# The final norm's two sums of squares: per-block matmuls with two columns instead of running sums on VectorE

## The chip, the cores and the metric

One core of a Trainium2 chip (trn2) runs the whole kernel. The metric is the device time of that core in microseconds (us). TensorE has two clock levels, 1.2 and 2.4 GHz; the profile shows as "granted clock" which share of full speed the chip allowed.

## The reference, cut to what matters

Two networks run one after the other on 1024 tokens of width 1024, all in fp32. The first has two attention layers and ends in a norm, with the gain `final_norm_gain`. The second starts with a norm of its own (`norm_mix_g_2`) ahead of a pooling mixer and a feed-forward part (FFN).

```python
def rmsnorm(x, g):
    y = xf * lax.rsqrt(jnp.mean(xf * xf, axis=-1, keepdims=True) + EPS)
    return (y * g).astype(x.dtype)
# first_block:  x = x + y @ w_out_odd[o];   return rmsnorm(x, final_norm_gain)
# second_block: h = rms_norm(x, norm_mix_g[0]);  x = x + pool_mixer(h, ...)
#               x = x + conv_ffn(rms_norm(x, norm_ffn_g[0]), ...)
```

Two norms follow directly on each other there. With r = 1/sqrt(mean(x^2) + eps), the second norm needs mean((x r g)^2) = r^2 mean((x g)^2). So the kernel takes two sums over the features of the same x: of x^2, and of (x g)^2, with g the final gain. "The final norm" below means this pair.

## The kernel before, in words

x lies transposed in SBUF: eight blocks `X[:, c, :]` of 128 features (partitions) by 1024 tokens. Most work is done in two halves of 512 tokens, n = 0 and n = 1. The weights come by DMA (queue SP) into a raw ring `WR`; ScalarE (ACT) rounds them to a high part and GpSimd (POOL) or VectorE (DVE) takes the low part (`split`, L2357), into a ring of six slots in `WS` and, late in the kernel, four more in `PT`. Each product takes three matmuls (high x high, high x low, low x high: L1534 to L1536).

A planner in Python writes one list, `steps`; each engine's program goes through this list in its order and issues its part of each step. So an instruction on an engine is always behind the engine's parts of all earlier steps. Side work is written as generators that are advanced by one `yield` for each piece of a matmul task ("pump"); a piece is mostly 6 matmuls.

The stretch around the change is `odd_tail`:

- Eight tasks `p1{oc}0` finish the output projection for n = 0 (12 matmuls each), then eight tasks `o1{oc}1` do it for n = 1 (36 matmuls each). After each, VectorE adds the product to X (L2036). They use PSUM banks 0 and 1 in turn, so the second next task waits for that addition.
- `rows_out` calls `square(fin[n], oc, ...)` one piece after task oc. For the final norm `fin[n]` that is two ScalarE squares of a 128x512 block: plain (`PY<-X`), and with the gain as scale (`PY<-X,COL`). Block 0 goes straight to two accumulators in `PY`; for blocks 1 to 7 each square goes to one of three slots `YS` and VectorE adds it to its accumulator (step `acc`, L2173). An `acc` is held back until the next call of `square` or the end. A slot of `YS` is free again once its `acc` is done.
- `close(fin[n])`: TensorE sums each accumulator over the partitions with a column of ones (step `sums`, L1707: 16 matmuls with the 128x128 piece of squares as weights and one column moving). VectorE and GpSimd work out both roots (L2180, L2346, L2186 to L2196), TensorE spreads them (`bcast`, L1721) into banks B_S+n and B_S+n+2 (B_S = 2).
- `mixed(n)` then runs the pooling mixer's blocks 0 to 7: `block sum` (L2246, L2253 or the scan L2255), `block diff` (L2269, L2271, L2273) on VectorE, `block split` on ScalarE, `block lo` (L2416) on GpSimd. `block sum` of block c waits for `block lo` of block c-2. `mixed(0)` goes beside the tasks `o1{oc}1`, `mixed(1)` beside the first FFN tasks. The pool products (`pool mm`) are tasks of 2 pieces between them; each of the eight blocks of a half gets one more ScalarE square and an `acc` for the FFN norm `ffn[n]`.
- The FFN begins with `half_task`s (24 matmuls). Each ends in `half leave`, in which ScalarE copies two columns to `TAIL` and scales the bank to a buffer `HBUF`; buffer 0 is PY[:, 1024:1536], which is also the second accumulator of half 0. Ahead of it ScalarE waits for `p.after`, a list that has the `sums` of `fin[1]` as the planner knows it when the step is written. Next come two VectorE instructions of `half conv` (L2282, L2288). For the first `half_task`, the planner has not yet closed `fin[1]`, so the value waited for there is 0. `close(fin[1])` follows one piece later.

Other norms (`x_norm`, `l1`, `ffn`, `mem_norm`) use the same functions with one sum each (`second` is None).

Of the kernel before, what the change touches and what calls it, by code (L numbers as in the profile page):

```python
# [9 lines left out]
ALU = mybir.AluOpType  # L10
# [55 lines left out]
class Norm:  # L66


    def __init__(self, src, n, stat, base, bank, second=None):
        self.src, self.n, self.stat, self.base, self.bank, self.second = src, n, stat, base, bank, second  # L70
        self.acc = [0, 0]
        self.var2 = self.var3 = self.rstd2 = 0
        self.sums = self.var = self.rstd = self.bcast = 0
        self.nd, self.nh, self.lo = [0] * 8, [0] * 8, [0] * 8
        self.col = self.ring = self.dst = None
        self.before = []
# [86 lines left out]
def build(nc, d):  # L163
    ctx = ExitStack()
    with ctx:
        def sb(name, shape, dt=F):
            return ctx.enter_context(nc.sbuf_tensor(name, shape, dt))
# [21 lines left out]
        ST = sb("ST", [128, 8, 4])  # L189
        RD = sb("RD", [128, 2, 2, 2])  # L190
        SK = sb("SK", [128, 8])
        PCT = sb("PCT", [128, 4, 16])
        SS = sb("SS", [128, 16])
        SM = sb("SM", [128, 16])
# [87 lines left out]
        s_score, s_mx, s_exp, s_sink, s_rec = (signal(n) for n in ("s_score", "s_mx", "s_exp", "s_sink", "s_rec"))  # L282
        s_turn, s_pth, s_ptl, s_pv = (signal(n) for n in ("s_turn", "s_pth", "s_ptl", "s_pv"))
        s_spread, s_yc, s_fin = (signal(n) for n in ("s_spread", "s_yc", "s_fin"))
        s_sq, s_acc, s_sums, s_var, s_pow, s_bcast = (signal(n) for n in ("s_sq", "s_acc", "s_sums", "s_var", "s_pow", "s_bcast"))
        s_nd, s_nh, s_nlp, s_nlv = (signal(n) for n in ("s_nd", "s_nh", "s_nlp", "s_nlv"))
        s_yh, s_ylp, s_ylv = signal("s_yh"), signal("s_ylp"), signal("s_ylv")
# [310 lines left out]
        def flush_acc():  # L598
            while held:
                put("acc", *held.pop(0))  # L600

        def square(nm, c, need):
            flush_acc()
            for j in range(1 if nm.second is None else 2):
                if c == 0:
                    put("square", nm, c, j, need, None, (s_turn, s_turn.n), (s_sums, s_sums.n))
                    nm.acc[j] = (s_sq, s_sq.add())
                    continue
                i = at["ys"] % 3
                at["ys"] += 1  # L610
                put("square", nm, c, j, need, i, ys_after[i], nm.acc[j])
                held.append((nm, j, i, s_sq.add(), nm.acc[j]))
                nm.acc[j] = ys_after[i] = (s_acc, s_acc.add())

        def close(nm):
            flush_acc()
            both = nm.second is not None
            nm.sums, nm.before_stat = s_sums.add(), s_bcast.n
            nm.var, nm.rstd = s_var.add(), s_pow.add()
            put("sums", nm)  # L620
            yield
            if both:
                nm.var2, nm.rstd2 = s_var.n, s_pow.add()
                s_var.add(3)
                put("second sums", nm)
                yield
                nm.var3 = s_var.add()
                put("second root", nm)
            yield
            nm.bcast = s_bcast.add()  # L630
            put("bcast", nm)
# [689 lines left out]
        def half_task(j, base, n):  # L1321
            p = Ffn("in", j, base, 0, 8, *add_units(in_units(d["ffn_in"], [(base + 128 * j, 128)])), halves=(n,))

            def leave_half():
                yield
                p.freed = s_fd.add(2 if n == 0 else 4)
                put("half conv", p, n)
                if base == 0:
                    return
                yield  # L1330
                yield
                p.silu = s_fa.add()
                put("half silu", p, n)
                yield
                p.product = s_fd.add()
                half_free[p.val.buf] = p.product
                put("half product", p, n)
                yield
                p.hi = s_fa.add()
                put("half hi", p, n)  # L1340
                yield
                half_free[p.buf] = s_fd.add()
                ut_at.setdefault(j, [0, 0])[n] = s_fd.n
                put("half lo", p, n)

            def gen():
                p.bank = (4, 6, 2, 0)[half_no[0] % (3 if n == 0 else 4)]
                p.buf = half_no[0] % 4
                half_no[0] += 1
                for i in range(len(p.tiles)):  # L1350
                    ahead(p.first + i)
                    if i == len(p.tiles) - 1:
                        p.mm[n] = s_fm.add()
                        used[p.first + i] = (s_fm, p.mm[n])
                    else:
                        used[p.first + i] = (s_wused, s_wused.add())
                    put("ffn mm", p, n, i)
                    if i < len(p.tiles) - 1:
                        yield
                p.at = 2 * j + (base > 0)  # L1360
                p.after = [(s_sums, fin[1].sums), sg_after[1], (s_fd, half_free[p.buf])]
                p.left = s_fa.add(2 if n == 0 else 1)
                put("half leave", p, n)
                if base == 0:
                    tail_val[n] = p
                else:
                    p.val = tail_val[n]
                defer(leave_half())
            tasks.append((f"half{j}{base}{n}", gen, 4))
# [42 lines left out]

        def odd_tail():
            none = iter(())
            at["deep"] = (at["split"], s_pv.n)
            for oc in range(8):
                rows_out(f"p1{oc}0", fin[0], oc, none)
            side = mixed(0)
            for oc in range(8):
                rows_out(f"o1{oc}1", fin[1], oc, side)  # L1420
            ht_after[1] = (s_mm, s_mm.n)
            state["mm"] = s_mm.n
            other = mixed(1)
            while "pool03" not in done:
                pump()
                next(side, None)
            while deferred:
                step_deferred()
            for _ in side:
                pass  # L1430
            while pump():
                next(other, None)
            for _ in other:
                pass
# [94 lines left out]
        def tensor_program(e):  # L1529
# [19 lines left out]
            for kind, *of in steps:  # L1549
# [146 lines left out]

                elif kind == "sums":
                    nm, = of
                    both = nm.second is not None
                    for j in range(2 if both else 1):  # L1700
                        w.wait_ge(*nm.acc[j])
                    w.wait_ge(s_init, 2)
                    w.wait_ge(*until[B_X])
                    for j in range(2 if both else 1):
                        for t in range(nm.n // 128):
                            a = 1024 * j + nm.base + 128 * t
                            m = e.matmul(PS[:, B_X, 4 * j + t:4 * j + t + 1], PY[:, a:a + 128], ON[:, :], start=True, stop=True)  # L1707
                    m.then_inc(s_sums.sem, 1)
                    until[B_X] = (s_var, nm.var2 + 1 if both else nm.var)

                elif kind == "bcast":
                    nm, = of
# [52 lines left out]
        def scalar_program(e):  # L1765
# [13 lines left out]
            for kind, *of in steps:  # L1779
# [120 lines left out]
                elif kind == "square":  # L1900
# [2 lines left out]
                    w.wait_ge(*need)  # L1903
                    if after is not None:
                        w.wait_ge(*after)
                    if c == 0:
                        w.wait_ge(*prev)
                        a = 1024 * j + nm.base
                        act(PY[:, a:a + nm.n], nm.src(c), ACT.Square, scale=scale).then_inc(s_sq.sem, 1)
                    else:  # L1910
                        act(YS[:, i, 0:nm.n], nm.src(c), ACT.Square, scale=scale).then_inc(s_sq.sem, 1)
# [53 lines left out]
                elif kind == "ffn leave":  # L1965
                    p, = of
                    if p.kind == "in":
# [3 lines left out]
                        w.wait_ge(s_fm, p.mm[1])  # L1971
                        w.wait_ge(s_sums, s_sums.n)
                        w.wait_ge(s_acc, s_acc.n)
                        w.wait_ge(s_pp, blocks[1, 7].lo)
                        w.wait_ge(s_fd, p.buf_free)
                        act(T, ps, ACT.Identity, bias=COL[:, C_CB + col:C_CB + col + 1],
# [10 lines left out]
        def vector_program(e):  # L1987
# [27 lines left out]
            for kind, *of in steps:  # L2015
# [159 lines left out]
                elif kind == "sums":  # L2175
                    nm, = of
                    st, nt = nm.stat, nm.n // 128
                    w.wait_ge(s_sums, nm.sums)
                    w.wait_ge(s_bcast, nm.before_stat)
                    e.tensor_scalar(st[:, 0:nt], PS[:, B_X, 0:nt], 1.0 / DM, EPS, ALU.mult, ALU.add).then_inc(s_var.sem, 1)  # L2180

                elif kind == "second sums":
                    nm, = of
                    st = nm.stat
                    w.wait_ge(s_pow, nm.rstd)
                    e.scalar_tensor_tensor(out=st[:, 8:12], in0=PS[:, B_X, 4:8], scalar=1.0 / DM, in1=st[:, 4:8],  # L2186
                                           op0=ALU.mult, op1=ALU.mult).then_inc(s_var.sem, 1)
                    w.wait_ge(s_var, nm.var2 + 1)
                    e.tensor_tensor(st[:, 8:12], st[:, 8:12], st[:, 4:8], ALU.mult).then_inc(s_var.sem, 1)
# [35 lines left out]
                elif kind == "last y":  # L2225
                    n, yh, _, _, _, _ = of
                    sl = slice(512 * n, 512 * n + 512)
                    w.wait_ge(s_yh, yh)
                    e.tensor_tensor(y_at(11, 1)[:, sl], SG[:, sl], f32(y_at(11, 0)[:, sl]), ALU.subtract).then_inc(s_ylv.sem, 1)

                elif kind == "pool columns":
                    w.wait_ge(s_exp, of[0])
# [378 lines left out]
```

## Time and profile before

| what | us |
|---|---|
| median of 3 runs | 2480.85 (2480.84 to 2481.98) |
| profiled execution, device time | 2480.93 |
| its span, first to last instruction | 2479.1 |
| TensorE (PE) busy | 2384.5 (96%) |
| VectorE (DVE) busy | 1285.7 (52%) |
| ScalarE (ACT) busy | 1207.7 (49%) |
| GpSimd (POOL) busy | 921.1 (37%) |
| mean granted TensorE clock | 0.992 |

The shares are means over the whole span. The final norm's work lies between 1612 and 1740 us, so it has to be read from that stretch. In a timeline a row gives the start (us), the duration (us), engine, line, operation, out<-in, shapes and xcount; in brackets stands how long the engine had been idle before it and who ended that. Most ScalarE instructions have the helper's line, L1769.

### The profile page before, as it was taken

What the parts mean: (1) busy time and instruction counts of PE and PEld (TensorE: products, weight loads), DVE (VectorE), ACT (ScalarE), POOL (GpSimd) and SP (SyncE); (2) the same over time, 40 slices, a digit from 0 to 9 for tenths busy, and PEclk for the clock granted to TensorE, in tenths of its full rate; (3) what the DMA queues carried; (4) which work ended last, traced back from release to release, by engine and by line L of the source; (5) the groups of instructions that cost most, each with busy time, mean ns of one, the idle gap of its engine ahead of it and who ended that gap; (6) DMA issues with size and microseconds to landing.
All of it is one profiled execution on the core that took longest, in us unless ns stands there. A gap on an engine that the chain in (4) does not pass through costs nothing.

```text
span 2479.1 us, 36148 instructions
## 1 busy us (share of the span) xinstructions
PE 2384.5 (96%) x12568; PEld 2017.7 (81%) x12568; DVE 1285.7 (52%) x2665; ACT 1207.7 (49%) x2873; POOL 921.1 (37%) x1133
## 2 busy tenths in 40 slices
PE   7999999999999999999999998999889999999999
PEld 6788787878878878888888887877778888888887
DVE  7344667667775333355555555587966213321331
ACT  6444566566775434455555565554554213322331
POOL 5554322311145642311222223577665323322321
PEclk9999999999999999999999999999999999999999
DMA  7322101111243332322223224432223211111112
GB/s 220 108 69 64 39 22 35 31 33 51 59 135 96 98 115 69 94 71 79 85 80 90 84 81 136 134 88 85 73 86 98 60 47 52 45 50 51 47 48 89
DMA packets 305987, 191.91 MB, mean 77 GB/s; under 512 B 63760, under 2 KB 284176, under 8 KB 305296
## 3 DMA queue, kind: packets, MB, share of 16 engines
q1 hardware_dynamic: 305808, 189.61, 26.0%
q8 instruction: 102, 1.67, 0.3%
q14 instruction: 77, 0.63, 0.1%
HBM read 170.16 MB, written 19.40 MB: 76 GB/s over the span
## 4 chain that ended last, share of the span: by engine, by line
PE 84%; DVE 5%; ACT 3%; issue 3%; POOL 3%; DMA 1%; SPq 1%; POOLq 0%; DVEq 0%; ACTq 0%
PE PS L1534 21%; PE PS L1536 21%; PE PS L1535 21%; PE PS L1680 5%; PE PS L1647 5%; PE PS L1634 3%; PE PS L1635 2%; PE PS L1691 2%; POOL WS L2357 1%; ACT PY L1769 1%; POOL HT L2416 1%; DVE EO L2209 1%; DVE ST L2099 1%; PE PS L1589 1%; PE PS L1671 1%
## 5 line engine op out<-in xcount | busy, mean ns | idle before, releaser
L2357 POOL TENSOR_TENSOR WS<-WR,WS 128x256 fp32r<-128x256 f32 x773 | 595.9, 790 | 1234.3 <-ACT WS L1769 1233.6
L1534 PE MATMUL PS<-HT,WS 128*128 128x512 f32 x1760 | 709.7, 403 | 31.9 <-POOL HT L2416 10.1
L1536 PE MATMUL PS<-HT,WS 128*128 128x512 f32 x1760 | 690.7, 392 | 0.0
L1535 PE MATMUL PS<-HT,WS 128*128 128x512 f32 x1760 | 689.2, 392 | 0.0
L1769 ACT ACTIVATE WS<-WR 128x256 fp32r<-128x256 f32 x788 | 296.1, 409 | 270.0 <-PE PS L1536 234.0
L1534 PEld LDWEIGHTS PS<-HT,WS 128*128 128x128 f32 x1760 | 333.5, 189 | 101.4 <-issue 14.6
L1536 PEld LDWEIGHTS PS<-HT,WS 128*128 128x128 f32 x1760 | 332.5, 189 | 72.5
L1535 PEld LDWEIGHTS PS<-HT,WS 128*128 128x128 f32 x1760 | 333.7, 190 | 63.0
L1769 ACT ACTIVATE PT<-PS 128x512 fp32r<-128x512 f32 x352 | 186.2, 529 | 229.9 <-PE PS L1647 229.7
L1992 DVE TENSOR_TENSOR PT<-PS,PT 128x512 fp32r<-128x512 f32 x352 | 211.2, 609 | 72.8 <-ACT PT L1769 70.0
L1680 PE MATMUL PS<-PT,QKV 128*128 128x256 f32 (+1 forms) x1248 | 207.3, 287 | 3.2 <-DVE YB L2163 2.2
L2357 POOL TENSOR_TENSOR PT<-WR,PT 128x256 fp32r<-128x256 f32 (+1 forms) x166 | 134.9, 828 | 202.3 <-ACT PT L1769 202.2
L1769 ACT ACTIVATE QKV<-PS 64x512 fp32r<-64x512 f32 (+2 forms) x208 | 121.7, 585 | 149.0 <-PE PS L1536 130.7
L1680 PEld LDWEIGHTS PS<-PT,QKV 128*128 128x128 f32 x1248 | 179.0, 191 | 10.6 <-ACT PT L1769 3.6
L1647 PE MATMUL PS<-ID,PY 128*128 128x128 f32 x1072 | 185.8, 277 | 0.0
L1534 PE MATMUL PS<-QKV,WS 128*128 128x512 f32 (+1 forms) x380 | 143.1, 377 | 7.5 <-DVE WS L2023 3.6
L1993 DVE SCALAR_TENSOR_TENSOR QKV<-PS,QKV 64x512 fp32r<-64x512 f32 (+1 forms) x112 | 77.2, 689 | 130.9 <-ACT QKV L1769 128.8
L1535 PE MATMUL PS<-QKV,WS 128*128 128x512 f32 (+1 forms) x380 | 141.7, 373 | 0.0
L1536 PE MATMUL PS<-QKV,WS 128*128 128x512 f32 (+1 forms) x380 | 141.6, 373 | 0.0
L1634 PE MATMUL PS<-QKV 128*128 128x384 f32 (+2 forms) x320 | 121.6, 381 | 14.4 <-ACT PY L1769 10.6
L1534 PE MATMUL PS<-HT,PT 128*128 128x512 f32 x320 | 126.5, 395 | 7.1 <-POOL WS L2357 4.2
L1647 PEld LDWEIGHTS PS<-ID,PY 128*128 128x128 f32 x1072 | 124.4, 140 | 10.9 <-issue 10.5
(192 smaller groups left out, 3717.5 us busy)
## 6 DMA issues: line engine op xcount, KB each, us to landing
WR<-in_ffn_in SPq DMA_DIRECT2D x120, 256.0 KB, 2.9
WR<-in_w_in_odd SPq DMA_DIRECT2D x106, 256.0 KB, 3.0
EO<-in_grid SPq DMA_DIRECT2D x48, 384.0 KB, 3.1
WR<-in_w_in_even SPq DMA_DIRECT2D x100, 128.0 KB, 2.5
WR<-in_w_out_odd SPq DMA_DIRECT2D x48, 256.0 KB, 2.9
yd<-PY SPq DMA_DIRECT2D x44, 256.0 KB, 2.9
WR<-in_w_in_even SPq DMA_DIRECT2D x34, 256.0 KB, 2.9
WR<-in_w_out_even SPq DMA_DIRECT2D x64, 128.0 KB, 2.8
```

The lines of the kernel that those rows point to most:

```text
L1534: e.matmul(out, wh, rh, start=start, stop=False)
L1535: e.matmul(out, wh, rl, start=False, stop=False)
L1536: return e.matmul(out, wl, rh, start=False, stop=stop)
L1634: e.matmul(out, q, kh, start=True, stop=False)
L1635: m = e.matmul(out, q, kl, start=False, stop=True)
L1647: m = e.transpose(PS[:, B_PT + pb, o + 128 * z:o + 128 * z + 128], p_at(job.c, job.scores[x].slot, p0, p0 + 128), ID[:, :])
L1680: m = e.matmul(out, vv, p, start=a, stop=b)
L1691: m = e.matmul(PS[n * h:n * h + n, B_X, 128 * x:128 * x + 128], RD[:, f.pp % 2, x, h:h + 1].to_broadcast([128, n]), ID[:, :], start=True, ...
L1769: return e.activation(out, in_, func, **more)
L1992: return e.tensor_tensor(out, src, f32(hi), ALU.subtract)
L1993: return e.scalar_tensor_tensor(out=out, in0=src, scalar=scale, in1=f32(hi), op0=ALU.mult, op1=ALU.subtract)
L2357: e.tensor_tensor(ws(i, 1, n), RAW[raw_slot(u)][:, o:o + n], f32(ws(i, 0, n)), ALU.subtract).then_inc(s_wlop.sem, 1)
```

## The change

For the final norm alone, the squares of a block are no longer scaled a second time and no longer added on VectorE. ScalarE squares each block once, into a slot of `YS` (block 0 too). TensorE then takes this block's four 128x128 pieces as weights against two moving columns, `GS[:, c, :]` = (1, g^2) for that block's features, and accumulates over the eight blocks in PSUM bank B_S+n: one column pair for each piece of 128 tokens. `sums` issues nothing more on TensorE for this norm; VectorE reads the pairs with a stride. A `square sum` is held back until the second next call of `square` for the final norm (`flush_sums(1)`), the next call for another norm, or `close` (`flush_sums(0)`). A slot of `YS` is free once its `square sum` is done. Two small VectorE instructions fill `GS` at the start of `odd_tail`. ScalarE's `half leave` waits for `fin[1].summed` in place of `fin[1].sums`; `summed` is set by each call of `square`, so at the first `half leave` it is the last block's `square sum`.

```diff
+        unsummed = []
+        def flush_sums(keep):
+            while len(unsummed) > keep:
+                put("square sum", *unsummed.pop(0))
+
         def square(nm, c, need):
+            if nm.sum_bank is not None:
+                flush_sums(1)
+                i = at["ys"] % 3
+                at["ys"] += 1
+                put("square", nm, c, 0, need, i, ys_after[i], None)
+                nm.summed = ys_after[i] = (s_sqm, s_sqm.add())
+                unsummed.append((nm, c, i, s_sq.add(), nm.blocks))
+                nm.blocks += 1
+                return
+            flush_sums(0)
             flush_acc()
...
         def close(nm):
             flush_acc()
+            flush_sums(0)
...
-                p.after = [(s_sums, fin[1].sums), sg_after[1], (s_fd, half_free[p.buf])]
+                p.after = [fin[1].summed, sg_after[1], (s_fd, half_free[p.buf])]
...
         def odd_tail():
             none = iter(())
+            for n in (0, 1):
+                fin[n].sum_bank = B_S + n
+            put("square columns")
+            s_cols.add(2)
...
                 elif kind == "sums":
                     nm, = of
+                    if nm.sum_bank is not None:
+                        continue
...
+                elif kind == "square sum":
+                    nm, c, i, squared, no = of
+                    both, bank = nm.second is not None, nm.sum_bank
+                    w.wait_ge(s_init, 2)
+                    if both:
+                        w.wait_ge(s_cols, 2)
+                    w.wait_ge(s_sq, squared)
+                    if no == 0:
+                        w.wait_ge(*until[bank])
+                    for t in range(4):
+                        out, x = (PS[:, bank, 2 * t:2 * t + 2], GS[:, c, :]) if both else (PS[:, bank, t:t + 1], ON[:, :])
+                        m = e.matmul(out, YS[:, i, 128 * t:128 * t + 128], x, start=no == 0 and t == 0, stop=no == 7 and t == 3)
+                    m.then_inc(s_sqm.sem, 1)
+                    until[bank] = (s_var, nm.var2 + 1 if both else nm.var)
...
+                elif kind == "square columns":
+                    w.wait_ge(d_const, 64)
+                    g = COL[:, C_FING:C_FING + 8]
+                    e.memset(GS[:, :, 0], 1.0).then_inc(s_cols.sem, 1)
+                    e.tensor_tensor(GS[:, :, 1], g, g, ALU.mult).then_inc(s_cols.sem, 1)
```

## Rows read from the trace of the kernel before

**Rows 1.** Page, part 4: the chain that ended last, by engine.
```profile
PE 84%; DVE 5%; ACT 3%; issue 3%; POOL 3%; DMA 1%; SPq 1%; POOLq 0%; DVEq 0%; ACTq 0%
```

**Rows 2.** Windows: length, busy PE, PEld, DVE, ACT, POOL, clock, DMA, GB/s.
```profile
1657.00:1681.00 24.00, 17.46 (x65) 13.18 (x64) 23.20 (x30) 13.04 (x27) 17.54 (x19) 0.86 0.20 57
1681.00:1720.00 39.00, 39.00 (x181) 32.54 (x180) 26.21 (x32) 20.03 (x44) 32.46 (x35) 1.00 0.33 95
...
1738.00:1800.00 62.00, 51.91 (x226) 41.80 (x225) 56.67 (x65) 35.62 (x83) 44.08 (x48) 0.97 0.24 69
...
1843.00:2479.00 636.00, 632.91 (x2784) 523.59 (x2784) 189.85 (x191) 179.39 (x352) 200.68 (x263) 1.00 0.20 59
```

**Rows 3.** Groups by line, 1612 to 1729: busy us, mean ns | idle before.
```profile
L2173 DVE TENSOR_TENSOR PY<-PY 128x512 f32<-128x512 f32 x35 | 34.2, 1016 | 0.6 <-ACT PY L1769 0.5
...
L1769 ACT ACTIVATE PY<-X 128x512 f32<-128x512 f32 x24 | 15.0, 623 | 9.3 <-DVE X L2036 8.9
...
L1769 ACT ACTIVATE PY<-X,COL 128x512 f32<-128x512 f32 x16 | 11.4, 714 | 5.7 <-DVE PY L2173 5.7
```

**Rows 4.** Timeline of TensorE around two `sums`, of 16 and of 8.
```profile
1631.95 1.84 PE L1707 MATMUL PS<-ON,PY 128*128 128x1 f32 x16
...
1633.65 0.49 PE L1534 MATMUL PS<-HT,WS 128*128 128x512 f32 x1
...
1633.97 0.40 PE L1535 MATMUL PS<-HT,WS 128*128 128x512 f32 x1
...
1707.78 0.95 PE L1707 MATMUL PS<-ON,PY 128*128 128x1 f32 x8
1708.59 0.49 PE L1534 MATMUL PS<-QKV,PT 128*128 128x512 f32 x1
```

**Rows 5.** Timeline of TensorE: matmuls that it waited for.
```profile
1658.41 0.50 PE L1534 MATMUL PS<-HT,PT 128*128 128x512 f32 x1 [0.78 <-DVE X L2036]
...
1674.99 0.79 PE L1534 MATMUL PS<-HT,WS 128*128 128x512 f32 x1 [5.41 <-DVE X L2036]
...
1678.27 0.76 PE L1534 MATMUL PS<-HT,PT 128*128 128x512 f32 x1 [0.35 <-DVE X L2307]
...
1725.12 0.50 PE L1534 MATMUL PS<-HT,PT 128*128 128x512 f32 x1 [1.45 <-DVE HT L2216]
...
1799.83 0.77 PE L1534 MATMUL PS<-HT,WS 128*128 128x512 f32 x1 [6.40 <-POOL HT L2416]
```

**Rows 6.** Timeline of VectorE, 1660 to 1678.
```profile
1660.85 2.32 DVE L2173 TENSOR_TENSOR PY<-PY 128x512 f32<-128x512 f32 x2
...
1666.28 1.28 DVE L2173 TENSOR_TENSOR PY<-PY 128x512 f32<-128x512 f32 x2
...
1671.93 0.75 DVE L2246 SCALAR_TENSOR_TENSOR EO<-X,ST,PS 128x512 f32<-128x512 f32 x1 [0.52 <-POOL HT L2416]
...
1674.28 0.66 DVE L2036 TENSOR_TENSOR X<-X,PS 128x512 f32<-128x512 f32 x1
...
1677.38 0.74 DVE L2307 SCALAR_TENSOR_TENSOR X<-PS,COL,X 128x512 f32<-128x512 f32 x1
```

**Rows 7.** Timeline of GpSimd, 1667 to 1672.
```profile
1667.50 2.50 POOL L2357 TENSOR_TENSOR PT<-WR,PT 128x256 fp32r<-128x256 f32 x2 [2.35 <-ACT PT L1769]
...
1670.10 1.80 POOL L2416 TENSOR_TENSOR HT<-EO,HT 128x512 fp32r<-128x512 f32 x1
```

**Rows 8.** Timelines of ScalarE, VectorE and TensorE, 1728 to 1737.
```profile
1728.09 0.78 ACT L1769 ACTIVATE PY<-PS,COL 128x512 f32<-128x512 f32 x1
...
1729.76 0.75 DVE L2288 SCALAR_TENSOR_TENSOR PY<-PS,COL,PY 128x510 f32<-128x510 f32 x1
1731.12 0.16 DVE L2180 TENSOR_SCALAR SS<-PS 128x4 f32<-128x4 f32 x1 [0.61 <-PE PS L1707]
...
1729.18 1.89 PE L1707 MATMUL PS<-ON,PY 128*128 128x1 f32 x16
...
1735.16 2.05 PE L1721 MATMUL PS<-ID,SS 128*128 128x128 f32 x16
```

More of the change, by code:

```diff
@@ L71, in __init__ @@
         self.acc = [0, 0]
+        self.sum_bank, self.summed, self.blocks = None, None, 0
         self.var2 = self.var3 = self.rstd2 = 0
-        self.sums = self.var = self.rstd = self.bcast = 0
+        self.var = self.rstd = self.bcast = 0
         self.nd, self.nh, self.lo = [0] * 8, [0] * 8, [0] * 8
@@ L191, in build @@
         SK = sb("SK", [128, 8])
+        GS = sb("GS", [128, 8, 2])
         PCT = sb("PCT", [128, 4, 16])
@@ L284, in build @@
         s_spread, s_yc, s_fin = (signal(n) for n in ("s_spread", "s_yc", "s_fin"))
+        s_cols, s_sqm = signal("s_cols"), signal("s_sqm")
         s_sq, s_acc, s_sums, s_var, s_pow, s_bcast = (signal(n) for n in ("s_sq", "s_acc", "s_sums", "s_var", "s_pow", "s_bcast"))
@@ L616, in close @@
             flush_acc()
+            flush_sums(0)
             both = nm.second is not None
-            nm.sums, nm.before_stat = s_sums.add(), s_bcast.n
+            if nm.sum_bank is None:
+                nm.summed = (s_sums, s_sums.add())
+            nm.before_stat = s_bcast.n
             nm.var, nm.rstd = s_var.add(), s_pow.add()
@@ L1698, in tensor_program @@
                     nm, = of
-                    both = nm.second is not None
-                    for j in range(2 if both else 1):
-                        w.wait_ge(*nm.acc[j])
+                    if nm.sum_bank is not None:
+                        continue
+                    w.wait_ge(*nm.acc[0])
                     w.wait_ge(s_init, 2)
                     w.wait_ge(*until[B_X])
[L1704 to L1707, printed above, removed]
+                    for t in range(nm.n // 128):
+                        a = nm.base + 128 * t
+                        m = e.matmul(PS[:, B_X, t:t + 1], PY[:, a:a + 128], ON[:, :], start=True, stop=True)
                     m.then_inc(s_sums.sem, 1)
-                    until[B_X] = (s_var, nm.var2 + 1 if both else nm.var)
+                    until[B_X] = (s_var, nm.var)
+                elif kind == "square sum":
[12 more added lines that the diff above has]
+                    until[bank] = (s_var, nm.var2 + 1 if both else nm.var)
                 elif kind == "bcast":
@@ L1905, in scalar_program @@
                         w.wait_ge(*after)
-                    if c == 0:
+                    if i is None:
                         w.wait_ge(*prev)
@@ L1973, in scalar_program @@
                         w.wait_ge(s_acc, s_acc.n)
+                        w.wait_ge(s_sqm, s_sqm.n)
                         w.wait_ge(s_pp, blocks[1, 7].lo)
@@ L2177, in vector_program @@
                     st, nt = nm.stat, nm.n // 128
-                    w.wait_ge(s_sums, nm.sums)
+                    w.wait_ge(*nm.summed)
                     w.wait_ge(s_bcast, nm.before_stat)
-                    e.tensor_scalar(st[:, 0:nt], PS[:, B_X, 0:nt], 1.0 / DM, EPS, ALU.mult, ALU.add).then_inc(s_var.sem, 1)
+                    ps = PS[:, B_X, 0:nt] if nm.sum_bank is None else PS[:, nm.sum_bank, 0:nt]
+                    if nm.second is not None:
+                        ps = PS[:, nm.sum_bank, 0:8].rearrange("p (t j) -> p j t", j=2)[:, 0, :]
+                    e.tensor_scalar(st[:, 0:nt], ps, 1.0 / DM, EPS, ALU.mult, ALU.add).then_inc(s_var.sem, 1)
                 elif kind == "second sums":
@@ L2185, in vector_program @@
                     w.wait_ge(s_pow, nm.rstd)
-                    e.scalar_tensor_tensor(out=st[:, 8:12], in0=PS[:, B_X, 4:8], scalar=1.0 / DM, in1=st[:, 4:8],
+                    ps = PS[:, nm.sum_bank, 0:8].rearrange("p (t j) -> p j t", j=2)[:, 1, :]
+                    e.scalar_tensor_tensor(out=st[:, 8:12], in0=ps, scalar=1.0 / DM, in1=st[:, 4:8],
                                            op0=ALU.mult, op1=ALU.mult).then_inc(s_var.sem, 1)
```

## The prediction

> **What bounds the kernel now.** I read the page's chain first: 84% of it is TensorE [rows 1]. From 1843 us to the end TensorE is busy 632.9 of 636.0 us [rows 2], so whatever shift reaches that point stays in the time. Then I asked where, near the change, TensorE is *not* the limit, and took the busy times by stretch [rows 2]. From 1681 to 1720 it is busy all 39.0 us: work added there is paid in full. From 1657 to 1681 it is busy only 17.5 of 24 us, at a mean granted clock of 0.86, while VectorE is busy 23.2 us: there VectorE and what hangs on it set the pace, and work added on TensorE may vanish. From 1738 to 1800 it has some 10 us of slack, which ends in a wait of 6.40 us for GpSimd's low part of the last pooling block [rows 5]. That stretch starts from the final norm's broadcast for half 1 (1735.16 us, [rows 8]), since each block's sum needs it. So the change of the time is the shift of that broadcast; what TensorE loses or gains between it and 1800 us is swallowed by the slack.
>
> **What goes and comes.** From VectorE go 28 of the 35 additions of the stretch (2 sums x 7 blocks x 2 halves; the other 7 belong to the FFN norm), 28 x 1.016 = 28.4 us [rows 3]. From ScalarE go all 16 scaled squares, 11.4 us, and 5.7 us in which it waited for a free slot [rows 3]. TensorE gets 16 groups of 4 small matmuls and loses 2 groups of 16. None of the removed work is on the chain except where VectorE is the limit, so it is not a gain of 28 us.
>
> **Price of a group on TensorE.** Sixteen `sums` lie between 1631.95 and 1633.65; the product after them is followed at 0.32 us instead of the usual 0.227 (36 matmuls of a task in 8.2 us): 1.70 + 0.10 = 1.80 us. Eight take 1708.59 - 1707.78 = 0.81, with the same 0.10 0.91 us [rows 4]. So one is 0.11 us, and a group of four about 0.48. The trace has no two-column matmul. Bounds: 0.42 (four at 1.70/16) from below, and from above 0.6, if each group were to pay the change of kind twice (0.91/2 + 0.10, rounded up). I take 0.48: sixteen broadcast matmuls with 128 moving columns take about the same 1.8 us as those with one (2.05 us with the last one's drain, against 1.89, [rows 8]), so a second column should be free.
> The Trainium skill, TensorE: Matmul & The Clock Gate, LDWEIGHTS (loading the stationary operand), speaks against the design: the load costs by the 128 columns of the weights, 128/1.2 = 107 ns, and here the squares are the weights. By that rule 48 more matmuls are 5.1 us; the same page's section "Wait — 56ns, not 53.3ns?" has matmuls follow at no less than about 25 ns however few columns move, by which alone they would be 1.2 us (an estimate, as the 5.1). The trace agrees with the first (0.106 us).
>
> **1. Half 0, up to its broadcast: +2.0 us.** TensorE has no gap from 1612 to 1657 that these groups could fill. Six groups (blocks 0 to 5) go among the tasks, 6 x 0.48 = 2.9; the last two stand in `close` in place of the 16 `sums`, 0.91 - 1.80 = -0.9. Their squares are done well before: a group is two tasks of 2.7 us behind its square, and a square needs the addition to X and 0.6 us. The two instructions that fill `GS` fall where VectorE idles.
>
> **2. The stretch 1657 to 1681: -3.8 us.** TensorE waits 0.78, 5.41 and 0.35 us, twice for the addition to X, once for a pool product's [rows 5]. The addition to X at 1674.28 is late because it stands in VectorE's queue behind a full row of pooling work and two pairs of the removed additions, 2.32 us at 1660.85 and 1.28 us at 1666.28 [rows 6]. Take the pairs out: block 4's difference ends 2.25 us earlier, so ScalarE splits it earlier, and the two weight splits behind that on ScalarE and GpSimd (2.50 us at 1667.50, which waited 2.35 us for ScalarE) and GpSimd's low part (1670.10) follow [rows 7]. All 3.6 us don't come through: block 6's sum at 1671.93 already waited 0.52 us for that low part [rows 6], and GpSimd's chain moves only by about 2.3 to 3.3. So the addition to X comes near 1671.5 instead of 1674.28. TensorE arrives there 0.9 us later (the groups of blocks 1 and 2; block 0's is swallowed by the 0.78) at 1670.5, waits about 1.6, then once more about 1.7 us for the pool product's addition, which is 3.1 to 3.8 us behind the addition to X (1674.28 to 1678.12 before). What is late next is thus again VectorE. The next task starts at 1675.3 instead of 1678.27. The mean clock 0.86 over 24 us is half speed for 6.8 us [rows 2]; it followed the wait of 5.41 and held for the first 1.6 us of that task, 0.8 us lost. With waits of 1.6 and 1.7 I expect no fall: 3.0 + 0.8 = 3.8. Bounds: 0 (GpSimd and ScalarE hold the chain as before), and 5.5 (all 3.6 us of the pairs, the 0.35, and the clock loss of all matmuls from 1675 on, less the 0.9 of groups).
>
> **3. Half 1, blocks 3 to 5: +1.4 us**, 3 x 0.48 in the full stretch to 1720.
>
> **4. First FFN piece, 1720 to 1728: -1.6 us.** TensorE waits 1.45 us at 1725.12 for a low part that VectorE [rows 5] had queued behind a pair of final-norm additions (some 1.3 us), and 0.3 for a weight split that ScalarE had behind a square waiting for a slot. Both go; the wait before (0.64, same chain, no addition ahead of it) stays. Bounds 0 and -2.4.
>
> **5. `close` and the first `half leave`: +1.5 us.** This is the added wait. ScalarE's activation at 1728.09 [rows 8] now waits for block 7's group, which TensorE has only after one more piece (6 matmuls) and eight small ones: `sums` stood at 1729.18 [rows 8], plus 0.85 is 1730.1. So the activation starts some 2.1 us later and ends at 1731.0; behind it VectorE's two `half conv` instructions end near 1732.6 instead of 1730.5 (1729.76 + 0.75), and in VectorE's queue behind these stands the first step of the roots, L2180: 1732.6 instead of 1731.12. From there to the broadcast is 4.04 us [rows 8]: 1736.65 instead of 1735.16. TensorE, 0.9 us quicker through `close`, waits there some 2.7 us. Bounds: -0.9 (the wait costs nothing) and +2.2. The weight splits behind the waiting activation are nine pieces ahead, so nobody waits for them.
>
> **Sum:** 2.0 - 3.8 + 1.4 - 1.6 + 1.5 = -0.5. The profiled execution had 2480.93 us (span 2479.1 and 1.8 around it), 0.08 above the median of the runs: 2480.4.
>
> **Rivals.**
> *A, faster: the relief is larger.* In 2 and 4 the additions and GpSimd may also slow each other: two additions last 2.32 us at one place and 1.28 at another, and they had GpSimd's low part beside them in the first case only [rows 6]. If GpSimd's chain gets quicker too, step 2 is -5.0, and if `half leave` is hidden step 5 is -0.9: 2.0 - 5.0 + 1.4 - 1.6 - 0.9 = -4.1, with both at their ends (-5.5, -2.4) -5.4: about 2475.9. For it: VectorE is busy 97% of that stretch. Against it: the queue order of step 5 is plain in the rows.
> The Trainium skill, GPSIMD Engine Reference, Key points, has GpSimd share its SBUF interfaces with VectorE's instructions of two SBUF inputs; the additions are such. The trace agrees in VectorE's lengths (2.32 against 1.28); it does not show GpSimd's own gain.
> *B, slower: TensorE's cost stays, the relief doesn't come.* If the pooling blocks are held by ScalarE and GpSimd rather than VectorE, TensorE waits as long as before in step 2 (0): 2.0 + 0 + 1.4 + 0 + 1.5 = +4.9 with step 4 at 0 too, 2485.8; with groups at 0.6 another +1. It is slower as soon as step 2 gives less than 3.3. For it: GpSimd's low part gates block 6 already. Against: these engines wait for VectorE in the rows.
> *C: the squares come too late, and the change puts a wait on TensorE* at each group of half 1 in place of VectorE's queue, 0.5 to 1 us each for four: +3, 2483.5. Against: a group is three pieces (4.1 us) or more behind its square.
>
> **How the numbers follow.** What a measurement can tell from no change is 0.2%, 5.0 us. Forecast and its neighbours (-4 to +4) 0.66, A 0.15, B 0.12, C 0.07. A's and B's own spreads reach both sides of the bounds 2475.9 and 2485.8: of A two thirds count as faster (0.10), of B two thirds as slower (0.08), of C 0.01; with the ends of the forecast's spread (0.07 and 0.05) it is faster 0.17, slower 0.14, same 0.69. The range 2475.0 to 2486.0 holds the forecast with its bounds, C, most of A and of B.
>
> **What would show it.** After: L2173 7 times in this stretch; groups of four small matmuls at 0.11 us each; the broadcast of half 0 later by 2 us; the 5.41 us wait under 3 and no fall of the clock there; ScalarE's first `half leave` idle for `square sum`, L2180 behind L2288, and TensorE waiting 2 to 3 us ahead of the half-1 broadcast. Wrong would be a wait of TensorE for a square, a group above 0.6 us, or a 1800 us wait whose end does not shift with the broadcast.

## The result, and the profile after

| | before | changed |
|---|---|---|
| median of 9 runs, us | 2481.43 (2477.45 to 2483.72) | 2489.26 (2485.60 to 2492.28) |
| span of the profiled execution | 2479.1 | 2488.9 |
| TensorE busy | 2384.5 | 2397.7 |
| VectorE busy | 1285.7 | 1261.8 |

The ratio is 1.0032, with a 95% interval of 1.0023 to 1.0041: some 8 us slower. Forecast was -0.5 us (2480.4), with a range of 2475.0 to 2486.0. The result is outside it.

The page's busy row (columns: engine, busy us, share, instructions) already shows what was wrong in the sum:

```profile
PE 2397.7 (96%) x12664; PEld 2031.6 (82%) x12664; DVE 1261.8 (51%) x2639; ACT 1198.2 (48%) x2857; POOL 913.7 (37%) x1133
```

TensorE has 96 instructions more than before (12568). The change adds 64 matmuls and takes 16 away, 48 more. So each of them is two instructions. (The large products, on rounded fp32r operands, are one row each: L1560, L1561 and L1562 follow in turn, as the code issues them.) The view of the added line says the same, 128 for 64 in the code (2 halves, 8 blocks, 4 pieces); its columns are duration min/median/max in ns, then the first and last start:

```profile
L1747 PEld LDWEIGHTS PS<-GS,PY x128: 187/192/192, 1618.0 to 1736.8; 128*128 128x128 f32 x128
L1747 PE MATMUL PS<-GS,PY x128: 165/251/251, 1618.3 to 1736.8; 128*128 128x2 f32 x128
```

Before, `sums` of the final norm were 8 matmuls a half, not the 16 that the description of the kernel before and the prediction took from "x16" [rows 4].

**A ruler.** The two executions already differ by 2.6 us ahead of the change, so I read shifts against a row that both have shortly before it, TensorE's restart after the last attention chunk:

```profile
1608.01 0.50 PE L1534 MATMUL PS<-QKV,WS 128*128 128x512 f32 x1 [0.89 <-DVE QKV L2229]
...
1637.87 2.05 PE L1721 MATMUL PS<-ID,SS 128*128 128x128 f32 x16
```

These are before; the second is the broadcast of half 0. The changed kernel's timeline of TensorE, where it answers to these and to [rows 4, 5, 8]:

```profile
1610.61 0.50 PE L1560 MATMUL PS<-QKV,WS 128*128 128x512 f32 x1 [0.85 <-DVE QKV L2274]
...
1618.27 0.95 PE L1747 MATMUL PS<-GS,PY 128*128 128x2 f32 x8
1621.94 0.95 PE L1747 MATMUL PS<-GS,PY 128*128 128x2 f32 x8
...
1646.16 2.04 PE L1761 MATMUL PS<-ID,SS 128*128 128x128 f32 x16
...
1680.20 0.50 PE L1560 MATMUL PS<-HT,WS 128*128 128x512 f32 x1 [0.57 <-DVE X L2077]
1683.48 0.47 PE L1560 MATMUL PS<-HT,PT 128*128 128x512 f32 x1 [1.63 <-DVE X L2358]
...
1715.01 0.95 PE L1732 MATMUL PS<-ON,PY 128*128 128x1 f32 x8
...
1735.21 1.84 PE L1747 MATMUL PS<-GS,PY 128*128 128x2 f32 x16
...
1743.47 2.77 PE L1761 MATMUL PS<-ID,SS 128*128 128x128 f32 x16 [2.18 <-DVE SS L2241]
...
1746.89 0.63 PE L1562 MATMUL PS<-HT,WS 128*128 128x512 f32 x1
...
1809.73 0.77 PE L1560 MATMUL PS<-HT,WS 128*128 128x512 f32 x1 [6.39 <-POOL HT L2467]
```

A task of 12 products with a group lasts 1621.94 - 1618.27 = 3.67 us; the products alone are 12 x 0.227 = 2.72, so a group is 0.95 us. Eight instructions with two moving columns (L1747) take the same 0.95 as eight with one (L1732). The wait of 5.41 us [rows 5] is 0.57 and the one behind it 1.63. The wait for the last pooling block, 6.39 us, is unchanged in length (6.40 before), and the times from its end to the end of the span are 679.27 before and 679.17 now. Whole runs of one kernel scatter by several us (2477.45 to 2483.72 before), so the shift at this wait is used below. Each kernel has one profile only; how little such shifts scatter is read from kernels that agree with each other.

Windows of the changed kernel (columns as in [rows 2]), for 1657 to 1681 and 1681 to 1720 there:

```profile
1660.00:1684.00 24.00, 21.80 (x107) 17.81 (x106) 22.43 (x29) 12.83 (x27) 21.39 (x22) 1.00 0.27 77
1684.00:1727.00 43.00, 43.00 (x210) 36.14 (x209) 22.01 (x27) 19.86 (x45) 31.57 (x36) 1.00 0.29 85
```

The first stretch has TensorE at full clock (0.86 before) and busy 21.8 us; VectorE is still at 93%. In its timeline the addition to X (L2077) has moved up, but stands behind block 6's sum, which again waits for GpSimd's low part; the pool products' additions (L2358) come next:

```profile
1677.13 0.75 DVE L2297 SCALAR_TENSOR_TENSOR EO<-X,ST,PS 128x512 f32<-128x512 f32 x1 [0.69 <-POOL HT L2467]
...
1679.49 0.65 DVE L2077 TENSOR_TENSOR X<-X,PS 128x512 f32<-128x512 f32 x1
...
1682.60 1.40 DVE L2358 SCALAR_TENSOR_TENSOR X<-PS,COL,X 128x512 f32<-128x512 f32 x2
```

Around the first `half leave`, ScalarE and VectorE of the changed kernel answer to [rows 8] (`<-issue` means that the profile shows nothing that ended the wait):

```profile
1737.14 0.17 ACT L1809 ACTIVATE TAIL<-PS 128x2 f32<-128x2 f32 x1 [4.77 <-issue]
1737.20 0.77 ACT L1809 ACTIVATE PY<-PS,COL 128x512 f32<-128x512 f32 x1
```
```profile
1738.80 0.75 DVE L2339 SCALAR_TENSOR_TENSOR PY<-PS,COL,PY 128x510 f32<-128x510 f32 x1
1739.46 0.15 DVE L2224 TENSOR_SCALAR SS<-PS 128x4 f32<-128x4 f32 x1
```

TensorE's sums ended near 1736.9 (1735.21 + 16 x 0.106). ScalarE starts right behind them, VectorE's conv instructions follow, and only then comes L2224, the first step of the roots: 2.5 us behind the sums, where before it was 0.2 us (1731.12 against 1729.18 + 16 x 0.106). That ScalarE waited for the sums is read from the code here; e1 tests it. TensorE waits 2.18 us for the roots.

### The profile page after: what moved, and what is told of

Same layout as the page of the kernel before. It is cut to its first block and busy times, and to the rows that moved or that the text cites. A ratio compares the mean times of both kernels' runs of the same rounds, so it can differ in the third digit from the quotient of the medians.

```text
span 2488.9 us, 36278 instructions
## 1 busy us (share of the span) xinstructions
PE 2397.7 (96%) x12664; PEld 2031.6 (82%) x12664; DVE 1261.8 (51%) x2639; ACT 1198.2 (48%) x2857; POOL 913.7 (37%) x1133
## 5 line engine op out<-in xcount | busy, mean ns | idle before, releaser
L1560 PE MATMUL PS<-HT,WS 128*128 128x512 f32 x1760 | 710.0, 403 | 27.7 <-POOL HT L2467 10.0
L1562 PE MATMUL PS<-HT,WS 128*128 128x512 f32 x1760 | 691.2, 393 | 0.0
L1561 PE MATMUL PS<-HT,WS 128*128 128x512 f32 x1760 | 689.5, 392 | 0.0
L1560 PEld LDWEIGHTS PS<-HT,WS 128*128 128x128 f32 x1760 | 333.8, 190 | 97.4 <-issue 15.3
L1562 PEld LDWEIGHTS PS<-HT,WS 128*128 128x128 f32 x1760 | 332.7, 189 | 72.6
L1561 PEld LDWEIGHTS PS<-HT,WS 128*128 128x128 f32 x1760 | 334.0, 190 | 63.0
L1560 PE MATMUL PS<-QKV,WS 128*128 128x512 f32 (+1 forms) x380 | 143.4, 377 | 7.6 <-DVE WS L2064 3.6
L1561 PE MATMUL PS<-QKV,WS 128*128 128x512 f32 (+1 forms) x380 | 141.7, 373 | 0.0
L1562 PE MATMUL PS<-QKV,WS 128*128 128x512 f32 (+1 forms) x380 | 141.6, 373 | 0.0
L1560 PE MATMUL PS<-HT,PT 128*128 128x512 f32 x320 | 126.3, 395 | 6.3 <-POOL WS L2408 4.1
```

The lines of the kernel that those rows point to most:

```text
L1560: e.matmul(out, wh, rh, start=start, stop=False)
L1561: e.matmul(out, wh, rl, start=False, stop=False)
L1562: return e.matmul(out, wl, rh, start=False, stop=stop)
```

## The experiments

Shifts in us against before, each from its own restart row as above (before: 29.86, 66.98, 127.15 and 191.82 us behind the row), and what whole runs gave. Restart rows lie between 1606.68 and 1610.61; from the last wait to the end the kernels take 679.2 to 681.7 us, e1 to e7 all 1 to 2.5 us more than before and changed. TensorE has the same 2956 instructions in that last part in all nine kernels, so I take the difference for scatter, and the column of the wait at 1800 for the sharper measure. Where half 0 is as before (e2, e5, e6, e7), its broadcast is within 0.03 us of before's.

| kernel | half-0 broadcast | end of the long wait near 1675 | half-1 broadcast starts | end of the wait at 1800 | ratio of runs (95%) |
|---|---|---|---|---|---|
| changed | +5.69 | +2.61 | +5.71 | +7.30 | 1.0032 (1.0023 to 1.0041) |
| e1, no leave wait | +5.64 | +2.57 | +3.33 | +3.39 | 1.0015 (1.0007 to 1.0024) |
| e2, half 1 only | +0.01 | -3.05 | +0.09 | +1.67 | 1.0006 (0.9997 to 1.0014) |
| e3, half 0 only | +5.69 | +5.68 | +5.07 | +5.08 | 1.0029 (1.0018 to 1.0040) |
| e4, small groups | +1.53 | -1.51 | +0.83 | +2.33 | 1.0001 (0.9991 to 1.0010) |
| e5, half 1, no leave wait | 0.00 | -3.08 | -2.33 | -2.36 | 0.9994 (0.9985 to 1.0003) |
| e6, e5 with spare additions | +0.02 | +0.26 | +3.62 | +2.98 | 1.0015 (1.0006 to 1.0024) |
| e7, half 1, blocks 0 to 2 | +0.03 | -3.04 | -3.84 | -3.89 | 0.9991 (0.9982 to 1.0000) |

**e1.** The leave no longer waits; nothing of the final norm is left in its buffers.

```diff
-                p.after = [fin[1].summed, sg_after[1], (s_fd, half_free[p.buf])]
+                p.after = [sg_after[1], (s_fd, half_free[p.buf])]
```

> The changed kernel, but ScalarE's half leave no longer waits for the final norm's sums (its buffers hold no accumulator of it any more). Theory: the change's +7.4 us are +5.5 for TensorE's groups of half 0, -3.8 of relief, +2.8 for blocks 3 to 5 of half 1, -1.2 of relief at 1730, +2.3 for ScalarE's wait at the first half leave and +1.6 for TensorE's late restart at half clock behind it. Without the wait the last two go: +3.5 us against before (2485 where before is 2481.4), and TensorE no longer waits ahead of the half-1 broadcast. Rival (the wait is hidden, all of the loss is TensorE's small matmuls): still +7 us.

The terms listed there add up to +7.2, and without the last two to +3.3.

The median was 2485.09, before 2482.07 beside it: +3.0. ScalarE goes ahead at once and TensorE has no wait ahead of the half-1 broadcast, which runs at full speed (2.05 us, against 2.77):

```profile
1731.10 0.17 ACT L1809 ACTIVATE TAIL<-PS 128x2 f32<-128x2 f32 x1 [1.66 <-PE PS L1562]
...
1738.19 2.05 PE L1761 MATMUL PS<-ID,SS 128*128 128x128 f32 x16
```

So the wait costs 7.30 - 3.39 = 3.9 us, 2.4 of them at the broadcast and 1.5 behind it.

**e2 and e3.** One half the new way, the other as before. The rest of the edit, not shown, puts back the old `sums` for the other half; the leave wait belongs to half 1, so e2 has it and e3 hasn't.

```diff
-            for n in (0, 1):
+            for n in (1,):        # e3: (0,)
                 fin[n].sum_bank = B_S + n
```

> Only the final norm of half 1 is summed block by block; half 0 keeps its two accumulators on VectorE. Theory: half 0's groups stand where TensorE has no gap and cost 6 x 0.92 = 5.5 us; without them -3.8 + 2.8 - 1.2 + 2.3 + 1.6 = +1.7 us against before, and the wait of 5.41 us near 1670 is below 1.5 us with no fall of the clock. Rival (the relief near 1670 was TensorE arriving later because of half 0's groups, not VectorE being quicker): the wait near 1670 stays above 4 us and the time is +4 us or more.

> Only the final norm of half 0 is summed block by block; half 1 keeps VectorE's additions. Theory: +5.5 us from half 0's groups and no relief: the wait of 5.41 us near 1670 stays, +5.5 us against before. Rival (the relief comes from half 0's late arrival): the wait near 1670 shrinks by some 3 us and the time is +2 us.

e2, TensorE: the long wait is gone though half 0's groups are not there; at 1733.92 the broadcast pays for the leave wait, and with 3.68 us for 2.05 for a fall of the clock.

```profile
1670.61 0.50 PE L1560 MATMUL PS<-HT,WS 128*128 128x512 f32 x1 [0.58 <-DVE X L2080]
...
1733.92 3.68 PE L1764 MATMUL PS<-ID,SS 128*128 128x128 f32 x16 [2.18 <-DVE SS L2246]
```

e3, TensorE: both waits of before stand to 0.01 us as in [rows 5].

```profile
1664.97 0.50 PE L1560 MATMUL PS<-HT,PT 128*128 128x512 f32 x1 [0.78 <-DVE X L2080]
...
1681.55 0.80 PE L1560 MATMUL PS<-HT,WS 128*128 128x512 f32 x1 [5.40 <-DVE X L2080]
```

The rival of both falls: the relief is half 1's own. Half 0 is pure cost: +5.1, where its six groups are 5.7. The median of its six whole runs is +6.8, more than either theory, with an interval of +4.5 to +9.9 that holds the 5.1. The two halves nearly add up: 1.67 + 5.08 = 6.75 against 7.30. The missing 0.6 is clock: behind the 5.40 us wait e3's TensorE goes at half speed for 3.8 us, where before it did for 5.1, and its shift falls from +5.68 to +5.07.

**e4.** Blocks 1 to 6 sum one piece of four; three quarters of the tokens lack these blocks' squares.

```diff
-                    for t in range(4):
+                    for t in range(4 if no in (0, 7) else 1):
```

> The changed kernel with one matmul instead of four in the groups of blocks 1 to 6 (three quarters of the tokens lack these blocks' squares). Theory (a matmul of these is two instructions of 0.11 us, a group 0.92 us): a group falls to 0.25 us; -5 x 0.67 in half 0 and -3 x 0.67 in half 1, together -5.4 us against the changed kernel, so +2 us against before. Rival (the price of a group is the change of kind between products and small matmuls, 0.1 to 0.3 us, and not the count): hardly any change, +6 us or more.

```profile
1618.06 0.28 PE L1747 MATMUL PS<-GS,PY 128*128 128x2 f32 x2
...
1672.23 0.50 PE L1560 MATMUL PS<-HT,WS 128*128 128x512 f32 x1 [1.94 <-DVE X L2077]
...
1675.51 0.77 PE L1560 MATMUL PS<-HT,PT 128*128 128x512 f32 x1 [1.00 <-DVE X L2358]
```

The price is the count: half 0's broadcast comes 5.69 - 1.53 = 4.16 us earlier, 0.69 for each of six groups (block 6 is one of them, which the expectation forgot). TensorE, now earlier, waits 1.94 us instead of 0.57 for the same addition, and 1.00 for the next. Unlike in the changed kernel, half speed follows (0.77 us for 0.47; granted clock 0.60 from 1675.5 to 1681). The ruler says +2.3 us as expected; the medians of whole runs are equal, with an interval of -2.2 to +2.5 that holds both.

**e5 and e6.** e5 is e1 and e2 together. e6 puts 14 additions back on VectorE where the final norm's stood, on a spare tile.

```diff
+                elif kind == "spare add":
+                    w.wait_ge(s_spare, of[0] - 1)
+                    e.tensor_tensor(F1[:, :], F1[:, :], F1[:, :], ALU.max).then_inc(s_spare.sem, 1)
```

> Both edits that helped together: block sums for half 1 only, and no wait of the half leave for the final norm. Theory: -3.8 + 2.8 - 1.2 = -2.2 us against before at the 1800 us wait (2480 where before is 2482). Rival (half 1 by itself gains nothing, its relief is eaten by its own groups): 0 or more.

> The half-1 kernel without the leave wait, with 14 additions of 128x512 put back on VectorE where the final norm's additions of half 1 stood; they work on a spare tile and nobody waits for them. Theory (the relief is VectorE's queue): the wait near 1670 is back at some 4 us, less the three groups that TensorE has by then, and the one at 1725; +5 us against the kernel without them, so +2.8 against before. Rival (the relief came from ScalarE's scaled squares, or from slots coming free earlier): no more than +1 us from the additions.

TensorE of e5, then of e6:

```profile
1674.41 0.50 PE L1560 MATMUL PS<-HT,WS 128*128 128x512 f32 x1 [0.57 <-DVE X L2080]
...
1725.36 0.50 PE L1560 MATMUL PS<-HT,PT 128*128 128x512 f32 x1 [0.25 <-DVE HT L2266]
```
```profile
1675.35 0.79 PE L1566 MATMUL PS<-HT,WS 128*128 128x512 f32 x1 [3.88 <-DVE X L2086]
...
1728.31 0.50 PE L1566 MATMUL PS<-HT,PT 128*128 128x512 f32 x1 [1.59 <-DVE HT L2272]
```

Both waits come back with the spare additions, 3.88 and 1.59, and with them half speed (0.79 us for 0.50) and 5.3 us. So the relief is VectorE's queue; ScalarE's scaled squares are absent in both and have no part. The size is a little high: the two pairs ahead of the first wait last 2.86 and 1.41 us, for 2.32 and 1.28 of those that they stand for [rows 6]. A last pair stands ahead of the roots, where before had none: TensorE waits 0.43 us ahead of the half-1 broadcast, with no fall of the clock, and that delay is gone at 1800 (+3.62, then +2.98). e5 alone is not told from before by its runs.

**e7.** As e5 (half 1 only, the first `half leave` waits for no sums), but TensorE sums only blocks 0 to 2, for which it has idle time; the rest go to VectorE's accumulators and join in the same bank at `close`. Parts of the edit:

```diff
-            if nm.sum_bank is not None:
+            if nm.sum_bank is not None and c < 3:
                 flush_sums(1)
...
-                if c == 0:
+                if c == (0 if nm.sum_bank is None else 3):
...
                     if nm.sum_bank is not None:      # in TensorE's "sums"
+                        w.wait_ge(s_cols, 2)
+                        for j in range(2):
+                            for t in range(4):
+                                a = 1024 * j + nm.base + 128 * t
+                                m = e.matmul(PS[:, nm.sum_bank, 2 * t + j:2 * t + j + 1], PY[:, a:a + 128], ON[:, :],
+                                             start=False, stop=j == 1 and t == 3)
```

> As the half-1 kernel without the leave wait, but only blocks 0 to 2 of half 1 are summed on TensorE, where it waits anyway; blocks 3 to 7 go to VectorE accumulators as before and join in the same bank at the close. Theory: the three groups in the full stretch go (-2.8), the relief at 1725 goes too (+1.2), the wait near 1670 stays short: -3.8 us against before, 1.6 better than the half-1 kernel. Rival (VectorE becomes late again after 1680): no better than it.

```profile
1673.48 0.50 PE L1559 MATMUL PS<-HT,WS 128*128 128x512 f32 x1 [0.56 <-DVE X L2087]
...
1722.77 0.50 PE L1559 MATMUL PS<-HT,PT 128*128 128x512 f32 x1 [1.46 <-DVE HT L2273]
...
1732.85 2.05 PE L1771 MATMUL PS<-ID,SS 128*128 128x128 f32 x16
```

The first wait stays short and the second is back, as expected; -3.9 us by the ruler, 2479.28 against 2481.84 by the medians. It is clearly better than the changed kernel (by 0.4%: ratios to before of 0.9991 and 1.0032, whose intervals don't meet). Against before its interval ends at 1.0000, so of that the ruler is the evidence more than the runs.

## Why the prediction was wrong, by its steps

**The price of a group** is the term that failed: 0.48 us forecast (bounds 0.42 to 0.6), 0.95 measured. I divided the time of the 16 rows in the trace by 16 and multiplied by the matmuls of the code, of which there are 8. The duration of a row was right (0.11), the unit was not. The xcount of 16, held against the loop in the code (2 sums x 4 pieces), would have shown it; the eight rows that were priced at 0.91 [rows 4] are four matmuls of the code, so the right price stood in the trace. With this price alone put right the forecast is +5.45 us, 2486.3, and already outside the range.

The other steps, with this one price put right:

| step | forecast | with a group at 0.95 | measured (ruler) |
|---|---|---|---|
| 1, half 0 | +2.0 | 6 x 0.95 = +5.7 | +5.69 |
| 2, 1657 to 1681 | -3.8 | -3.8 | 5.69 to 2.61, and 0.8 of clock: -3.9 |
| 3, blocks 3 to 5 | +1.4 | +2.85 | 1.8 to 4.6: +2.8 |
| 4, 1720 to 1728 | -1.6 | -1.6 | -1.2 |
| 5, close and leave | +1.5 | +2.3 | 3.43 to 5.71: +2.3 |
| behind the broadcast | 0 | 0 | +1.6 |
| sum | -0.5 | +5.45 | +7.3 |

The shifts for steps 3 and 4 come from TensorE's rows at 1729.21 (+4.61; 1722.00 before) and 1735.21 (+3.43; 1729.18 before). The 0.8 of clock is what is left of 2.61 to 4.61 when three groups are taken at 0.95.

**Step 1** also had `close` 0.9 us cheaper; the last two groups are 16 instructions and so were the sums. No gain, no loss.

**Step 2** was right in place and size, though partly by luck: the cost of three groups that it swallowed was 2.8 us and not 1.4, and the waits were 0.57 and 1.63 for 1.6 and 1.7. Not TensorE's arrival but the chain from the half-0 broadcast set the restart, VectorE's queue with GpSimd's low part in it: counted from that broadcast it is 3.04 to 3.08 us earlier than before in all of changed, e1, e2, e4, e5 and e7. The clock did not fall. That GpSimd would let only part through was right (0.69 us of wait for its low part).

**Step 4:** the wait of 1.45 us went to 0.27. The 0.3 us wait for a weight split stayed (0.28), so it wasn't the slot that ScalarE had waited for.

**Step 5** had the mechanism right: ScalarE's leave, VectorE's two conv instructions, L2224, the broadcast; its length was short by 0.8 us, near the 0.9 us that eight more rows take.

**What was missing** is the +1.6 behind the broadcast, a second step that failed. I held that TensorE's own delay after it is swallowed by the slack before 1800. Here it is not: block 0's split on ScalarE stands in its queue behind the third `half leave`, which waits for TensorE. ScalarE before, then changed:

```profile
1742.72 0.17 ACT L1769 ACTIVATE TAIL<-PS 128x2 f32<-128x2 f32 x1 [2.30 <-PE PS L1536]
...
1743.98 0.63 ACT L1769 ACTIVATE HT<-EO 128x512 fp32r<-128x512 f32 x1
```
```profile
1752.67 0.17 ACT L1809 ACTIVATE TAIL<-PS 128x2 f32<-128x2 f32 x1 [2.31 <-PE PS L1562]
...
1753.92 0.63 ACT L1809 ACTIVATE HT<-EO 128x512 fp32r<-128x512 f32 x1
```

The split is 7.34 us later from the restart row, though the broadcast was 5.71. Between them TensorE ran at half speed (the broadcast in 2.77 us, a product's 0.63 us at 1746.89 against 0.39 at full speed; mean granted clock 0.80 from 1743.4 to 1752). e2 shows the same (+0.09 to +1.67, the broadcast in 3.68 us), and e1 and e5, which have no wait there, have neither (3.33 to 3.39; -2.33 to -2.36). That the third `half leave` is the way is read from these rows; no run moves it alone. In e6 the split is 3.61 us late and the wait at 1800 ends 2.98 late, so 0.6 us can still go between them, and where is open.

Two of the prediction's own signs of being wrong came: a group above 0.6 us, and an end of the wait at 1800 that does not shift with the broadcast (7.30 and 5.71).

**Rivals.** B had the sign, but not the cause: the relief that it doubted came in full, and TensorE's cost was double. A had a true part. GpSimd of the changed kernel, for the first and the last row of [rows 7]:

```profile
1673.23 2.00 POOL L2408 TENSOR_TENSOR PT<-WR,PT 128x256 fp32r<-128x256 f32 x2 [1.21 <-ACT PT L1809]
...
1675.80 1.30 POOL L2467 TENSOR_TENSOR HT<-EO,HT 128x512 fp32r<-128x512 f32 x1
```

From the start of the splits to the end of the low part it takes 3.87 us, for 4.40 before, and as block 6's sum waits for that low part, 0.5 us of the 3.1 came this way. That the additions had slowed it is not shown: with the spare additions back, e6 takes 3.90 us there. The total is no larger than forecast. C did not happen: TensorE never waits for a square.

Two bounds don't follow from their terms: A's end is 2480.85 - 5.4 = 2475.5 and not 2475.9, and C's is 2483.4 and not 2483.5. Neither changes what the result says.

**The page's rule for loads.** The 107 ns per load of the Trainium skill, TensorE: Matmul & The Clock Gate, LDWEIGHTS (loading the stationary operand), is borne out per instruction: 0.106 to 0.119 us in these rows. By that rule and the two loads per fp32 matmul that the rows show, the 48 added are 10.3 us, an estimate near the 11.6 of the measured prices (16 x 0.95 less two `sums` of 1.80). The floor of about 25 ns for matmuls with few columns, which the same page of the Trainium skill gives in the section "Wait — 56ns, not 53.3ns?", is not reached here.

## What to carry to other kernels

Before a duration from a trace is multiplied by a count from the code, hold the row's xcount against the loop: here a plain fp32 matmul is two rows, and that alone put the sum some 6 us too low. Moving work to the engine that bounds the kernel paid here only where that engine waits: the same edit gained 3.9 us in one stretch and lost 5.7 in another, so apply it block by block (e7). And a semaphore wait that is kept "for safety" on a reused buffer should be asked what it still protects: this one protected nothing and cost 3.9 us.

## What the runs showed of the hardware

A two-column fp32 matmul costs what a one-column one does (0.95 us for eight instructions, both), and the two instructions of such a matmul take 0.11 to 0.12 us each. A wait of TensorE of 2.2 us ahead of the half-1 broadcast was followed by half speed, the lower of its two clock levels, in all three kernels that had it (changed, e2, e4: 2.77, 3.68 and 3.55 us for a broadcast of 2.05, granted clock 0.80, 0.79 and 0.78 in the 7 to 9 us from its start). Waits of some 0.6 and 1.63 us near 1675 were followed by none in the changed kernel, e1, e2, e5 and e7, but in e4, where the two were 1.94 and 1.00 us, half speed followed.
